# Scaling and rounding a pooled part on POOL between its products, in place of ScalarE between its sigmoids

## What is computed

```python
pooled = jnp.stack(groups, axis=2)      # trailing means of u over windows 2, 4, 8, 16, less u
mixed = jnp.einsum("btgc,gcd->btgd", pooled, w_pool_l).reshape(b, t, c)
pool_out = mixed * scale_l
...
z = jnp.einsum("bqhd,bkhd->bhqk", q_blk, k) * SB_SCALE
mask = k_pos[None, :] < q_pos[:, None]
log_1mb = jnp.where(mask, jax.nn.log_sigmoid(-z), 0.0)
log_a = jax.nn.log_sigmoid(z) + lax.cumsum(log_1mb, axis=3, reverse=True) - log_1mb
a = jnp.where(mask, jnp.exp(log_a), 0.0)
sb = jnp.einsum("bhqk,bkhd->bqhd", a, v)
...
mixed = jnp.concatenate([pool_out, sb], axis=-1)
mix_out = mixed @ w_o
```

## Time and profile before

| | us |
|---|---|
| median of 3 runs | 2582.84 |
| lowest and highest | 2579.41, 2584.56 |
| the profiled execution | 2587.18 |
| its span, first to last instruction | 2585.5 |
| attention stage in it, about | 486 to 1000 |

### The profile page before, as it was taken

The page is one execution under the profiler, slowest core; times in us unless marked ns, Lnnn a source line. Parts: engine busy times, 40 slices in busy tenths (PEclk is TensorE's granted clock), DMA queues, the critical chain, the costliest instruction groups (busy, mean ns, idle before and its releaser), DMA issues.

```text
span 2585.5 us, 36302 instructions
## 1 busy us (share of the span) xinstructions
PE 2431.2 (94%) x14328; PEld 1349.6 (52%) x14328; DVE 1415.9 (55%) x1861; ACT 1018.5 (39%) x1555; POOL 892.8 (35%) x1061
## 2 busy tenths in 40 slices
PE   4899899899998889999999999899999999999998
PEld 3445455444444444454565665345666544688733
DVE  4747665488888887889655554415333302433214
ACT  1522233499999895324443442102222200133200
POOL 1300000277777773333556556501111250111100
PEclk8899999899999999999999999999999999999999
DMA  7315868332332112222556566654454445476555
GB/s 249 100 50 171 283 235 272 120 99 82 99 84 81 34 66 93 78 94 84 165 179 212 179 198 234 227 196 155 155 163 131 139 138 180 153 224 203 186 164 167
DMA packets 216387, 395.63 MB, mean 153 GB/s; under 512 B 30189, under 2 KB 152365, under 8 KB 207642
## 3 DMA queue, kind: packets, MB, share of 16 engines
q1 hardware_dynamic: 199226, 331.45, 40.1%
q10 hardware_dynamic: 16992, 61.87, 7.7%
HBM read 302.97 MB, written 90.30 MB: 152 GB/s over the span
## 4 chain that ended last, share of the span: by engine, by line
PE 58%; DVE 9%; ACT 4%; POOL 4%; DMA 3%; issue 3%; SPq 0%; POOLq 0%; DVEq 0%; ACTq 0%
PE ps L2457 20%; PE ps L2497 15%; PE ps L2426 12%; PE ps L2361 3%; DMA dn_dram<-work 3%; DVE work L1709 3%; PE ps L2236 2%; POOL work L880 2%; PE ps L2213 2%; PE ps L2252 2%; ACT ps L1188 2%; ACT work L1176 2%; DVE work L1866 1%; DVE work L1706 1%; DVE work L1456 1%
## 5 line engine op out<-in xcount | busy, mean ns | idle before, releaser
L2457 PE MATMUL ps<-hidden_t,work 128*128 128x384 f16 (+1 forms) x3696 | 515.2, 303 | 1.9 <-ACT work L1307 1.1
L2497 PE MATMUL ps<-work 128*128 128x512 f16 x2244 | 472.5, 380 | 8.5 <-DVE work L1964 5.9
L2457 PEld LDWEIGHTS ps<-hidden_t,work 128*128 128x128 f16 x3696 | 361.4, 98 | 155.7 <-ACT work L1307 1.7
L2120 PE MATMUL ps<-hidden_t,work 128*128 128x416 f16 x1920 | 353.6, 345 | 14.2 <-DVE hidden_t L1474 10.0
L2426 PE MATMUL ps<-hidden_t,work 128*128 128x384 f16 x2112 | 347.6, 328 | 4.1 <-DVE work L1921 4.1
L2497 PEld LDWEIGHTS ps<-work 128*128 128x128 f16 x2244 | 206.4, 98 | 274.0 <-issue 29.8
L880 POOL TENSOR_TENSOR work<-work 128x512 f32<-128x512 f32 (+2 forms) x320 | 306.8, 965 | 112.4 <-DVE work L1709 63.9
L2426 PEld LDWEIGHTS ps<-hidden_t,work 128*128 128x128 f16 x2112 | 207.5, 98 | 144.3 <-issue 9.6
L2120 PEld LDWEIGHTS ps<-hidden_t,work 128*128 128x128 f16 x1920 | 190.3, 99 | 164.8 <-issue 17.8
L1709 DVE TENSOR_TENSOR_SCAN work<-ps,work 128x512 f32<-128x512 f32 x192 | 237.4, 1270 | 35.2 <-ACT ps L1188 34.3
L841 POOL TENSOR_TENSOR work<-work,col 128x1 f32<-128x1 f32 x68 | 33.2, 488 | 586.2 <-DVE work L1459 586.2
(11 more groups left out here) (243 smaller groups left out, 2723.5 us busy)
## 6 DMA issues: line engine op xcount, KB each, us to landing
work<-dn_dram ACTq DMA_DIRECT2D x96, 512.0 KB, 3.6
work<-gs_dram SPq DMA_DIRECT2D x88, 512.0 KB, 4.2
work<-gs_dram SPq DMA_DIRECT2D x44, 768.0 KB, 4.3
work<-in_w_ada SPq DMA_DIRECT2D x24, 1024.0 KB, 5.7
work<-in_w_gu SPq DMA_DIRECT2D x46, 512.0 KB, 7.1
work<-in_w_gu SPq DMA_DIRECT2D x22, 1024.0 KB, 5.9
gs_dram<-work SPq DMA_DIRECT2D x22, 1024.0 KB, 5.7
gs_dram<-work SPq DMA_DIRECT2D x66, 256.0 KB, 2.4
```

The source lines that it names most:

```text
L2120: mm = pe.matmul(ps[:, blk, 0:PB], B_HL[s][:, wh * KD * P + k * P:wh * KD * P + (k + 1) * P], hidden_t[:, k, xh, PB * blk:PB * (blk + 1)], ...
L2457: mm = pe.matmul(ps[:, bank, 0:n], E_GS[j % 2][:, GS_AT[q], wh, k, :], hidden_t[:, k0 + k, xh, at:at + n], start=(q in (1, 2, 5) and k == ...
L2497: mm = pe.matmul(ps[r:r + rows, 2 * slot + half, :], E_HID[:, j, xh, at:at + rows], E_DHL[slab_home(g)][:, wh, 512 * half:512 * (half + 1) ...
```

## The change

The 20 pieces of `pool_high` leave ScalarE's queue and are put into POOL's as a multiplication of `C_POOL` by the column C_SMIX with f16 output (tensor_scalar), at the same numbers of steps: in a step of POOL's loop the piece comes after the step's product and ahead of a `head_split` of that step. POOL's loop reads C_SMIX, so a wait for mix_set stands ahead of the loop. The semaphores pool_in and pool_hi are the same, and VectorE's `pool_low` isn't touched.

```diff
+            def pool_high(g, q):
+                pool.wait_ge(pool_in, 16 * (g + 1))
+                if q < 4:
+                    at = slice(BLK * q, BLK * (q + 1))
+                else:
+                    at = slice(SEQ, TOK)
+                pool.tensor_scalar(hidden_t[:, g, 0, at], C_POOL[:, at], c1(C_SMIX), None, ALU.mult).then_inc(pool_hi, 1)
+
+            pool.wait_ge(mix_set, 1)
             blk = 0
             for m in range(NTILE + 12):
                 if m < NTILE:
                     product(m)
+                h, at = m // (4 * NU), m % (4 * NU)
+                if h < NH and h % 2 == 0 and 21 <= at < 31 and at % 2 == 1:
+                    pool_high(h // 2, (at - 21) // 2)
                 if m >= 11 and ends_block(m - 11):
                     head_split(blk, min(m + 1, NTILE))
                     blk += 1
...
-            def pool_high(g, q):
-                act.wait_ge(pool_in, 16 * (g + 1))
-                if q < 4:
-                    at = slice(BLK * q, BLK * (q + 1))
-                else:
-                    at = slice(SEQ, TOK)
-                act.activation(hidden_t[:, g, 0, at], C_POOL[:, at], ACT.Identity, scale=c1(C_SMIX)).then_inc(pool_hi, 1)
-
...
-                if h < NH and h % 2 == 0 and 21 <= at < 31 and at % 2 == 1:
-                    pool_high(h // 2, (at - 21) // 2)
```

## The result

The changed kernel takes 2600.19 us (median of 6 runs, 2599.13 to 2601.11), the kernel before 2582.20 us beside it (6 runs); the ratio is 1.0061, with a 95% interval of 1.0051 to 1.0071. That is +15.8 us by the ratio (13.2 to 18.3), +18.0 by the medians. The forecast was +5.75 us, with a range up to 2595. The direction was right, the size was not, and the time lies outside the range. One execution of eight of v4_spread_early took 3469 us at a mean granted clock of 0.68 and is left out of its numbers; every other execution had 0.975 to 0.983.

What follows compares the result with a forecast made beforehand. The prediction took a ring of ScalarE, VectorE, POOL and TensorE as the bound. Start 3.15, three heads at 0.18 and the seventh head's 2.06 gave +5.75 us on the median 2582.84, so 2588.6 us; range 2582.5 to 2595.

Steps and rivals of the forecast that it cites:

- ring: Attention stage: ScalarE, VectorE, POOL, TensorE and ScalarE again wait for each other in a circle, nobody far ahead.
- The ceiling of 9 us: Most the change could gain: 2.24 us between heads with and without the pooled part, over four heads.
- ScalarE was the only bound: Rival, 7%: POOL has time, pooled heads become like their neighbours; -5.8 us, 2577 us.
- The piece's price: Cost of one 128x512 scaling on POOL: 0.70 us, plus 0.08 us between instructions.
- the upper end: Rival, 23%: a piece costs like a two-input product, 1.09 to 1.2 us; +9.7 us, 2592.5 us.
- the prediction's own formula: Whole added time in us for a piece's cost c: 5.75 + 10 x (c - 0.70).
- an even head: Each of three heads with a pooled part, the seventh and its extra steps apart: +0.18 us.
- The walk through a head: Third head: POOL's pieces delay VectorE's low halves 1 and 3; scan 30 moves from 663.27 to 663.45.
- Its slope of 3: Head with pooled part: 0.3 us per 0.1 us of piece price, as pieces 1, 2 and 3 lie on the path.
- Head 6: Seventh head: low half 1, VectorE's small steps for the final scales and scan 26 all come behind piece 1; +2.06 us.
- The start: Stage's start: the mix_set wait holds POOL's first select and configuration; product 0 moves from 493.57 to 496.7, +3.15 us.
- The rival that the load isn't held: 10%: at the stage's start the new wait doesn't delay the load, the start term falls away; +2.6 us, 2585.4 us.

Runs made afterwards that it cites:

- v4_spread_early: Changed kernel: broadcast-product pieces and low halves at other steps (head 0's first two pieces later still), wait before first piece, POOL's code loaded early; ratio 0.9970, median 2577.20 us.
- c1_round_only: Changed kernel with the scaling left out: POOL only converts each piece of C_POOL to f16; ratio 1.0012 to the kernel before, +3.1 us.
- t1_two_inputs: Changed kernel with each piece as a two-operand product of C_POOL and the column broadcast over the piece; ratio 1.0042 to the kernel before.
- v2_spread_column: Changed kernel, same instruction, pieces after products 3, 7, 16, 18, 20, low halves after scans 6, 12, 20, 24, 26, mix_set wait before first piece only; ratio 0.9995.
- l1_low_later: Changed kernel with VectorE's low halves four steps later each (27, 29, 31, 33, 35); ratio 1.0038 to the kernel before, head 2 at 65.42 us.
- e1: Changed kernel, mix_set wait kept, plus a single-element POOL product ahead of the attention stage to load its code early; ratio 1.0032, head 0 at 66.25 us.
- f1_prices: Kernel before plus a row of single POOL instructions behind its last step, run twice over; one run, only its trace read, stage 503.4 us.
- s1_early_load: Kernel before plus a single-element POOL product ahead of the attention stage to load its code early; ratio 0.9991, stage 499.3 us, 4.1 less.

## Why the prediction was wrong, step by step

**What bounds.** Right as a ring, wrong in what it allowed. The ceiling of 9 us came from setting heads with and without the pooled part side by side; their difference contains ScalarE's high and VectorE's low halves. The prediction said so and still priced the rival "ScalarE was the only bound" with all of it. Taking the high halves away showed 4.2 us.

**The piece's price: the step that failed.** 0.70 us was taken, 1.09 to 1.2 held for the upper end; it is 1.56. The bounds were drawn by the number of inputs. The rows at hand held a conversion and a two-operand product, none of a multiplication by a scalar, and it does not lie between them. In the prediction's own formula, 5.75 + 10 x (1.56 - 0.70) = 14.4 us, against 14.8 measured in the stage. That this close is in part luck. By the formula an even head would take 2.8 us more (measured 3.45), the seventh 2.9 (2.42), and the start 3.15 (2.5), and at the lower prices it gives 4.75 and 9.15 us where the stages of c1_round_only and t1_two_inputs were 2.6 and 8.3 us longer (all three with a load 0.7 to 0.8 us shorter than in the trace of the kernel before): the stage grows by 12.5 to 13 us for each us of price, not by 10. The range left out an instruction dearer than both of its neighbours. Price and place act together: at 0.60 us a piece these places cost nothing, and at 1.56 us other places cost nothing (head 2 at 63.31 us in v2_spread_column, 63.94 before).

**The walk through a head.** Right in its mechanism for VectorE: VectorE's waits before low halves 1 and 3, product 23 back from 1.53 to 1.08 us, VectorE as the path. Checked at 0.60 us a piece it met scan 30 within 0.1 us. Its slope of 3 was too small, 3.3 to 4.2, since piece 0 too comes onto the path, and the low halves are not the only ones who wait: TensorE's turn does, as l1_low_later showed.

**Head 6.** Forecast +2.06, and +2.9 at the real price; measured +2.42. Low half 1 did start 3.3 us later in the head (45.81 us after its first sigmoid against 42.49). Of the small steps behind it, one shrank from 0.87 to 0.19 us: a step with two inputs on VectorE, which had run while POOL did a product. From low half 1 to scan 26 it was 3.57 us before and is 2.77 now. The prediction had not looked at what stretched those steps, and took one for one with a piece's cost, which t1_two_inputs shows not to hold.

**The start.** Forecast +3.15, measured +2.5 from the first sigmoid to product 0, with a load of 6.8 us that was 0.7 shorter by itself. The select moved as computed (3.2 us later after the first sigmoid, 3.97 against 0.77), and e1 shows that it is the load which costs. The rival that the load isn't held is refuted: the configuration came at 488.9, behind the wait.

**The extra microseconds.** The stage explains 14.8 of the 15.8 us of the ratio (18.0 by the medians); the rest of the 15.8 is inside its interval and has no cause shown.

## What to carry to other kernels

Don't bound an unknown instruction by the number of its inputs: a kind that the trace doesn't show can be dearer than both of its neighbours, and where the sum moves by ten times the unknown, the range has to say so. Before moving work from a busy engine, ask where the receiving engine has room: the same five pieces cost nearly nothing, or 3.4 us a head, by their place, and a wait put at the head of a loop costs what it holds back, here a load of about 7 us. The difference between two otherwise equal stretches of one trace is a ceiling for everything they differ in, not for the part that a change moves.

## What the runs showed of the hardware

- On POOL a multiplication of 128x512 f32 by a scalar took 1.49 us (constant) and 1.57 us (column), a product of the same with the column broadcast as second operand 1.04 us, a conversion 0.61 us in the second pass and 1.08 in the first (f1_prices). The Trainium skill (GPSIMD Engine Reference, Engine selection) calls one-input work on POOL roughly line rate; beside VectorE's one-input step of 0.72 us on as many elements (L1729 in the changed kernel) the conversion agrees at 0.61, the multiplication by a scalar, one input as well, does not.
- After POOL's change of configuration its first product came 6.7 to 7.8 us later in all sixteen traces; in the four where it was asked for while POOL was idle, it cost nothing at the start of the stage, which was worth 4.1 us there (s1_early_load).
- VectorE's two-input steps and POOL's instructions lengthened each other, in both directions: product 23 took 1.53 us beside a low half and 1.08 without, low half 3 took 1.57 us beside POOL's product in the changed kernel and 0.73 in the one before, and a step of one column 1.03 us beside a piece (t1_two_inputs) and 0.15 without.
